# Where in an attention step TensorE issues the preceding step's value products

## The reference

```python
for blk in range(s // Q_BLOCK):
    qs, qe = blk * Q_BLOCK, (blk + 1) * Q_BLOCK
    sc = jnp.einsum('bhqd,bhkd->bhqk', qh[:, :, qs:qe], kh[:, :, :qe]).astype(jnp.float32) * scale
    ...
    pr = jax.nn.softmax(sc, axis=-1).astype(vh.dtype)
    outs.append(jnp.einsum('bhqk,bhkd->bhqd', pr, vh[:, :, :qe]))
```

## Time and profile before

| | us |
|---|---|
| median of 3 runs | 3404.64 |
| lowest, highest | 3404.55, 3409.43 |
| span of the profiled execution | 3401.4 |
| TensorE busy in it | 3301.1 (97%) |
| VectorE busy | 1848.6 (54%) |
| GpSimd busy | 1385.9 (41%) |
| ScalarE busy | 1113.3 (33%) |

### The profile page before, as it was taken

One profiled execution on the slowest core, in us unless ns is written; L12 is line 12 of the kernel. 1 busy time (PEld: TensorE's weight loads), 2 busy tenths in 40 slices (PEclk: granted clock), 3 DMA queues, 4 the chain that ended last, 5 costly groups with the idle time before them and its releaser, 6 DMA issues.

```text
span 3401.4 us, 44063 instructions
## 1 busy us (share of the span) xinstructions
PE 3301.1 (97%) x16322; PEld 2611.0 (77%) x16322; DVE 1848.6 (54%) x2928; ACT 1113.3 (33%) x1836; POOL 1385.9 (41%) x691
## 2 busy tenths in 40 slices
PE   9999999999999999999999999999999999999998
PEld 7888877778888788887777888887776666777676
DVE  5532378875433464234888643335545648575753
ACT  4222234422222422223443222223234642344332
POOL 4444454444444344444544444443242223322342
PEclk9999999999999999999999999999999989999999
DMA  5333332244433334333313443344642222322221
GB/s 147 93 116 92 106 88 66 60 122 135 131 89 110 102 120 146 88 102 95 81 44 101 127 133 91 94 155 124 212 131 60 59 57 68 60 46 69 84 86 50
DMA packets 632956, 335.01 MB, mean 98 GB/s; under 512 B 97774, under 2 KB 622703, under 8 KB 631247
## 3 DMA queue, kind: packets, MB, share of 16 engines
q1 hardware_dynamic: 608062, 286.80, 30.4%
q10 hardware_dynamic: 23680, 44.32, 3.6%
q0 software_dynamic: 1040, 1.57, 0.1%
HBM read 308.65 MB, written 23.98 MB: 98 GB/s over the span
## 4 chain that ended last, share of the span: by engine, by line
PE 83%; DVE 11%; issue 3%; ACT 2%; POOL 0%; DVEq 0%; DMA 0%; ACTq 0%; POOLq 0%
PE ps L345 25%; PE ps L334 25%; PE ps L346 24%; PE ps L1138 2%; PE ps L1172 1%; PE ps L1162 1%; DVE UH L440 1%; PE ps L520 1%; DVE TURN L449 1%; DVE UL L443 1%; DVE ps L864 1%; DVE UL L855 0%; DVE SS L452 0%; DVE PRE L385 0%; PE ps L1289 0%
## 5 line engine op out<-in xcount | busy, mean ns | idle before, releaser
L270 POOL TENSOR_TENSOR WL<-RAW,WH 128x1024 fp32r<-128x1024 f32 (+4 forms) x606 | 1297.3, 2142 | 1977.3 <-ACT WH L292 1976.7
L345 PE MATMUL ps<-UH,WH 128*128 128x512 f32 x3056 | 1218.5, 399 | 48.1 <-DVE UL L855 16.4
L346 PE MATMUL ps<-UL,WH 128*128 128x512 f32 x3056 | 1195.8, 391 | 0.0
L292 ACT ACTIVATE WH<-RAW 128x1024 fp32r<-128x1024 f32 (+4 forms) x605 | 571.0, 945 | 1170.6 <-PE ps L334 1126.7
L334 PE MATMUL ps<-UH,WL 128*128 128x512 f32 x3056 | 802.7, 394 | 0.7 <-POOL WL L270 0.7
L345 PEld LDWEIGHTS ps<-UH,WH 128*128 128x128 f32 x3056 | 574.5, 188 | 206.5 <-issue 43.9
L334 PEld LDWEIGHTS ps<-UH,WL 128*128 128x128 f32 x3056 | 570.0, 187 | 132.9 <-issue 12.5
L346 PEld LDWEIGHTS ps<-UL,WH 128*128 128x128 f32 x3056 | 574.8, 188 | 121.4 <-issue 4.5
L345 PE MATMUL ps<-HH,WH 128*128 128x512 f32 x704 | 273.9, 389 | 0.0
L346 PE MATMUL ps<-HL,WH 128*128 128x512 f32 x704 | 273.9, 389 | 0.0
L385 DVE TENSOR_TENSOR PRE<-ps,R 128x512 f32<-128x512 f32 x144 | 99.4, 691 | 293.1 <-PE ps L334 289.4
(11 more groups left out here) (447 smaller groups left out, 3441.1 us busy)
## 6 DMA issues: line engine op xcount, KB each, us to landing
RAW<-w_ff_in SPq DMA_DIRECT2D x176, 512.0 KB, 3.8
RAW<-w_in SPq DMA_DIRECT2D x72, 512.0 KB, 3.9
RAW<-w_ff_out SPq DMA_DIRECT2D x64, 384.0 KB, 3.4
RAW<-w_ff_out SPq DMA_DIRECT2D x64, 320.0 KB, 3.1
RAW<-d_w_in SPq DMA_DIRECT2D x24, 512.0 KB, 3.8
CM<-cm_dram ACTq DMA_DIRECT2D x8, 1088.0 KB, 10.5
RAW<-b_w_in SPq DMA_DIRECT2D x17, 512.0 KB, 3.7
RAW<-w_out SPq DMA_DIRECT2D x16, 512.0 KB, 3.8
```

Source lines behind the costliest of these rows:

```text
L270: e.tensor_tensor(m.WL[:, s, 0:k, :], m.RAW[:, r, 0:k, :], m.WH[:, s, 0:k, :].bitcast(F32), ALU.subtract).then_inc(m.low_ready.sem, 1)
L292: e.activation(m.WH[:, s, 0:k, :], m.RAW[:, r, 0:k, :], ACT.Copy).then_inc(m.high_ready.sem, 1)
L345: e.matmul(out, m.WH[:, s, c, 0:t.cols], H[:, k0 + c, :], start=(x == 0 and c == 0), stop=False)
L346: e.matmul(out, m.WH[:, s, c, 0:t.cols], L[:, k0 + c, :], start=False, stop=False)
```

## The change

In `Heads.tensor`, which the three kinds of attention share, the part that issues the values of pair s-3 moves from the end of step s to its beginning, ahead of the scores of step s and the turns of pair s-2. Its two waits move with it. The order on the other engines stays, and so does the number of steps taken at each place of the projections.

```diff
         for s in range(self.pairs + lag + 1):
-            if s < self.pairs:
-                self.scores(e, s)
-            if lag <= s < self.pairs + lag:
-                for a in (2 * (s - lag), 2 * (s - lag) + 1):
-                    h, n = self.block(a)
-                    e.wait_ge(m.normed.sem, self.b + a + 1)
-                    if self.b + a > 1:
-                        e.wait_ge(m.turned.sem, self.b + a - 1)
-                    for j in range(self.blocks(n)):
-                        mm = e.transpose(m.ps[:, 4 + a % 2, j * P:(j + 1) * P], self.buf.S[:, a % 4, j * P:(j + 1) * P], m.IDENT[:])
-                    mm.then_inc(m.flipped.sem, 1)
             if s >= lag + 1:
                 a = 2 * (s - lag - 1)
                 e.wait_ge(m.turned.sem, self.b + a + 2)
...
                         if j == nb - 1:
                             mm.then_inc(m.valued.sem, 1)
+            if s < self.pairs:
+                self.scores(e, s)
+            if lag <= s < self.pairs + lag:
+                for a in (2 * (s - lag), 2 * (s - lag) + 1):
+                    h, n = self.block(a)
+                    e.wait_ge(m.normed.sem, self.b + a + 1)
+                    if self.b + a > 1:
+                        e.wait_ge(m.turned.sem, self.b + a - 1)
+                    for j in range(self.blocks(n)):
+                        mm = e.transpose(m.ps[:, 4 + a % 2, j * P:(j + 1) * P], self.buf.S[:, a % 4, j * P:(j + 1) * P], m.IDENT[:])
+                    mm.then_inc(m.flipped.sem, 1)
             yield
```

## The result

The changed kernel takes 3437.6 us (median of 4 runs, 3433.13 to 3439.22) against 3404.68 us before. The ratio is 1.0095, with a 95% interval of 1.0082 to 1.0107: 33 us slower. The forecast was 3448.2 us, with a range of 3411 to 3463. In the changed file the values stand at L1161 and the turns at L1174 (before: L1172 and L1162); the other lines are the same.

The account below looks back on a forecast made before the run. TensorE, busy 3301.1 of 3401.4 us, was taken as the bound. Losses of 0.9 + 9.2 + 3.6 + 9.1 + 10.8 + 6.0 = 39.6 us, plus 4 for the clock, on 3404.6 gave 3448.2 us, range 3411 to 3463.

Parts of the forecast that it names:

- What bounds the kernel: Whole kernel: TensorE, busy 3301.1 of 3401.4 us, has little idle time to win; its own queue counts.
- The first block: Both layers: copies early in 30 of 32 pairs; only pair 5 waits, 0.5 us per layer, about 0.9 us.
- The sliding window, woven part: Steps among projections: nine pairs lose 9.2 us waiting for copies, pairs 13, 21, 23 and 24 together 3.6 us.
- The sliding window, tail: Four steps with no projection between them: pairs 25 to 29 lose 9.1 us, with the granted clock at 0.50.
- The latent layer, woven part: Six pairs after short tiles lose 6.2 us, the pairs after them 4.2, pair 0 0.4; together 10.8 us.
- the shift: Attention steps: values ahead of scores start the chain to the copies later by their length, 0.35 to 1.05 us.
- The latent tail: Latent steps with no projection between: pairs 25 to 30 wait for copies, 6.0 us in sum.
- The clock term: Latent tail: more standing may drop TensorE's clock to 1.2 GHz, 4 to 7 us if so, else 0; 4 taken.
- The values fill TensorE's idle time: Rival, mainly later attention steps: copies ready by the step's start, 12.0 us of waits go, 3392.6 us; 6%.
- Only the raw lateness: Third rival, attention steps: values don't delay the chain, VectorE's evictions hold it; 23 us, 3428, band 3411 to 3435; 20%.
- Hidden anyway: Rival, whole kernel: same cycle, delay taken back by engines running ahead in the projections; 3400 to 3410 us; 6%.
- The clock swings: Rival, woven parts: idles make TensorE's clock swing; +33 us on the 40, 3478, up to 3510; 7%.

Follow-up runs that it names:

- e2: Changed kernel with ScalarE's copies of a step put ahead of its exponentials, values still first on TensorE; 3386.1 us, 0.9943 of the kernel before.
- e7: Changed kernel with each of ScalarE's copies cut into pieces of 64 columns; 3468.4 us, 1.0186 of the kernel before.
- e5: Kernel before, with the new order in the two layers of the first block only; 3398.8 us, 0.9983 of the kernel before.
- e1: Changed kernel with the values issued between scores and turns in every step; 3416.4 us, 1.0031 of the kernel before.
- e9: Kernel before, with the new order only in steps 28 to 34 of the latent layer; 3412.6 us, 1.0024 of the kernel before.

## Why the prediction was right, and where it was off

**What bounds the kernel**: right. TensorE's waits in the four later stages grew by 35.2 us. That its busy time stayed the same in sum is chance: fewer changes of shape took some 8 us from the time outside waits, and the clock of the latent tail added 8.8.

**The first block**, +0.9: the wait was right (0.47 us at pair 5, once per layer, as worked out), and the sum was wrong in sign, -3.7, because I gave the transitions between scores, turns and values no price. The step that failed is "it adds and removes no instruction": the order changes how often TensorE changes the shape of its operands, and that costs 0.17 us each time. The rows with 0.17 were in the trace of before and I had not read them. The signs named for the first block were off with it: 0.5 us of waits in each layer and not some 1, and stretches 1.9 us shorter that were to stay as long.

**The sliding window, woven part**: the waits of pairs 1 to 23 grew by 12.8 us (1.7 to 14.5), and 12.0 were forecast for them, with 0.8 for pair 24. Pair 12 has 0.96 where 0.98 was worked out. The match of the sums hides misses of single pairs: pair 5 waits 1.52 us and pair 18 only 0.60, where 0.92 to 1.09 was given for both, and pairs 14 and 22 wait 0.6 us each, for which nothing was. The sum was 4 us too high for the same missing term, about 25 steps at 0.17 us.

**The sliding window, tail**: +9.6 for 9.1, nearly all waits (+9.4). The clock was low there before and after, and its price in the chain of values was in the sum. The sign to look for, about 20 us of waits of values in the whole stretch, didn't follow from that sum: the 21.9 us of both parts are net of old waits of 5.2, so some 27 had to stand there, and 27.4 did.

**The latent layer, woven part**: +7.3 for 10.8. A pair after a short tile costs 0.76 and not 1.03, the next 0.65 and not 0.7 (from one projection matmul to the next in the alignment). The choice not to add the shift in the first of the two was right: with it the sum would have been 1.8 us for that pair. The wait of such a pair is 1.27 us (1.03, and the 0.34 that TensorE had stood there for exponentials, make 1.37): the 0.10 between them is mostly the way from the copy's end to TensorE, 0.06 us and not 0.2. The other 0.17 lies outside the wait. It is as much as one change of shape, but the count of changes is the same in both orders, so that this is the cause isn't shown. Pair 0 cost 0.1 and not 0.4.

**The latent tail**: 6.0 for the waits, of which 4.3 came. The clock term, 4 us, is the one that was mis-sized most: time outside waits grew by 8.8. The direction had been taken from the nearer of two rows, and that was right; the size took two or three steps at half speed, and the fall lasted for 24 us, all steps of the tail.

**The rivals.** "The values fill TensorE's idle time" failed at the point named for it: the copies end after the step's start. "Only the raw lateness" would have been 23 us of waits; the waits of the four later stages grew by 12.8 + 9.4 + 8.7 + 4.3 = 35.2 us. So the chain does shift, and e2 shows that the shift is harmless when the copies are early. "Hidden anyway" is out by the same 35.2 us. "The clock swings" didn't happen in the changed kernel, and did in e7. The sum of 43.6 came out at 34.4 between the profiled runs (33 between the medians) because of the changes of shape (4.6 us in the first block, about 4 in the sliding window) and the cheaper latent pairs (3.5), with the latent tail going the other way by 3. That the errors had both signs kept the total as near as it is: the missing term for changes of shape alone, some 8 us, is larger than the distance of 3437.6 from the edge of the third rival's band, 3435.

## What to carry to other kernels

When a loop over steps has stages that follow one another in a cycle, moving one of them from the end of a step to its beginning changes only which stage has the other engine's work as its cover. So compare, step by step, the end of what the moved stage reads with the start of the step, and add what the move itself delays. Before giving such an order up, look at the engine that makes the operand: here it made the copies behind its longer work while it stood idle ahead of them, and with those two swapped the same order of TensorE was 18.5 us faster than the kernel before (some 5 of them with the clock), though either change alone made it slower. Count the changes of operand shape of an order on TensorE as well; they are in the trace, 0.17 us each.

## What the runs showed of the hardware

A change between whole-array, 64-row and 64-column operands costs TensorE about 0.17 us (first block and sliding window in the changed kernel and e2, the first block in e5, the sliding window in e1), and a mask matmul over the whole array between scores and values is enough to pay it twice there and not once (first block of e1). Between 96-row and whole-array operands no gap stands (latent layer, before and after).

Short stalls can bring TensorE's clock down to the 1.2 GHz level though no stall around the fall is longer than 2.3 us (changed kernel, latent tail: 24 us at 0.5), 1.9 us (e9: 17 us), 2.1 us (e7: six pieces in the latent layer's woven part) or 1.6 us (e1: 3.4 us in the sliding window's); in the same places the kernel before has no fall. The price is not the length of the fall by itself. In the changed kernel's latent tail, 24 us at 0.5 cost 8.8 us outside the waits. The sliding window's tail was at 0.5 for none of its time in e2, for 13.7 us before and for 23.9 after, and its time outside waits was 18.5, 23.5 and 23.7 us: what the low level cost there, some 5 us by e2, had been paid before the change. What exactly decides the fall wasn't settled by these runs.
